# Expert weights in nine slots instead of six, three experts deep

## The chip, the cores and the metric
The kernel runs on one core of one Trainium2 chip. The metric is the device time in microseconds of one execution. Three runs of the kernel before took 3150.36, 3154.68 and 3155.96 us, median 3154.68 us.

## The reference, cut to what matters
The program computes two blocks over 512 tokens of width 1024, all in float32. The first block is a mixer (dilated attention and retention) followed by a mixture of experts: 8 groups of 8 experts, each token sent to 2 experts of one group. The second block has two more layers, which this change does not touch. The part that the change concerns is this:

```
hn = rms_norm(h, norm_moe_w)
group_p = softmax(hn @ w_group + b_group);  g_w, g_idx = top_k(group_p, 1)
exp_logits = hn @ w_expert + b_expert       # 64 experts, the 8 of the chosen group count
e_w, e_idx = top_k(softmax(sel_logits), 2)
...
hid = silu(xb @ w1[e]) * (xb @ w3[e])       # w1, w3: 1024 x 512
y   = hid @ w2[e]                           # w2: 512 x 1024
out = segment_sum(y * gate)                 # then added to h
```

Each expert has three weight matrices of 2 MB each (2048 KB), so all 64 experts together have 192 matrices.

## The kernel before, in words
The program is a sequence of stages. At the end of each stage TensorE, VectorE and ScalarE report with `next_stage`, GpSimd collects the reports and increments `stage_open`, and only then do the engines go on. SyncE (SP) is outside this: it issues nearly all weight loads, in one order written out by hand, and each load waits for semaphores of its own. SP stops at the first wait that is not yet fulfilled, and every later load stands behind it.

The stages around the change are these. The *rest* stage ends the mixer: its last two weight units, 22 and 23 (`w_out`), are multiplied on TensorE (line 1239), `h` is normed tile by tile, and ScalarE stores the normed tiles to `normed_rows` in DRAM (line 1208). A unit of weights lies in two of the four ring slots, even units in slots 0 and 2, odd units in 1 and 3; `release_unit` increments `unit_used` when TensorE has done with one. `stage_open` is 6 when the *route* stage opens and 7 when the *experts* stage opens. In the route stage VectorE picks the two experts of each token in a long chain of small operations (lines 1451 to 1534), with a short piece on TensorE; GpSimd scatters a table of slots to DRAM (line 1546), and ScalarE reads it back (line 1438).

In the experts stage each expert is computed for up to 32 rows. GpSimd gathers the rows by an indirect DMA (`gather`, issued two experts ahead, line 1620) and scatters the results (line 1625). TensorE transposes the rows (line 1656), multiplies by w1 and w3 (line 1664, `up_product`), then does the down product of the expert *before* (line 1680, w2), the transpose of the next rows, and the transposes of the hidden values (line 1671). The order inside the body of expert e is therefore: up e (w1, w3), down e-1 (w2), transpose rows of e+1, transpose hidden of e.

The weights are in `wide`, six slots of 2 MB, two experts deep: expert e uses slots 3*(e%2)+j for j = 0, 1, 2 (w1, w3, w2). Slots 0 to 3 lie in the same place as the ring, slot 4 is `xn`, slot 5 is `xnT`. SP issues in the order e, j (line 1611):

- slots 0 to 3 (all of expert 0 and w1 of expert 1) after `unit_used` 24, that is when the last ring unit has been used, and `rows_sent`;
- slots 4 and 5 after `stage_open` 7;
- from then on w1 of e waits for `pair_used` 2e-3 (the first w3 product of expert e-2), w3 of e for `pair_used` 2e-2 (the transpose of rows after it), and w2 of e for `down_used` e, which is incremented at the hidden transposes in the body of expert e-1, after the down product of e-2.

As w2 of e stands in front of w1 and w3 of e+1 in SP's order, and its wait is fulfilled last, the three loads w2 of e, w1 of e+1, w3 of e+1 leave together, at the hidden transposes in the body of expert e-1. In what follows this is called the burst. At that time the loads that are still under way are those of the burst before, which were issued one expert earlier.

All engines run `turns`: four bodies written out, then a loop of 15 turns with four bodies each. The stage's work buffers are in `arena`: the route stage's (class `G`) first and the experts' (class `E`) behind them.

Of the kernel before, what the change touches and what calls it, by code (L numbers as in the profile page):

```python
# [18 lines left out]
F32 = mybir.dt.float32  # L19
# [7 lines left out]
P = 128  # L27
D = 1024
# [107 lines left out]
def build(nc, t, const, out):  # L136
    ctx = ExitStack()
    with ctx:
# [14 lines left out]
        expert_loaded = [sem(f"expert_loaded{i}") for i in range(6)]  # L153
# [54 lines left out]
        with ExitStack() as plain:  # L208
            wide = plain.enter_context(nc.sbuf_tensor("wide", [P, 6, UNIT], F32))
# [1171 lines left out]

        class G:
            lay = Arena(arena)
# [28 lines left out]
            empty = lay(2 * BLOCKS).bitcast(I32)  # L1412

# [139 lines left out]
        U_EXPERTS = 24  # L1553
        PAR = 4
        SLOTS = 6
        assert 3 * PAR % SLOTS == 0 and U_EXPERTS % RING == 0 and EXPERTS % PAR == 0

        class E:
            lay = Arena(arena)
            lay.at = G.lay.at  # L1560
            table = lay(2 * BLOCKS).bitcast(I32)
            index = lay(4, 2).bitcast(I32)
            x = lay(2, D)
            xT = lay(2, KC, CAP)
            gate = lay(HID)
            up = lay(HID)
            gate_sum = lay(FC, CAP)
            up_sum = lay(FC, CAP)
            silu = lay(FC, CAP)
            hT = lay(FC, CAP)  # L1570
            y = lay(2, D)
# [13 lines left out]
        def turns(eng, body):  # L1585

            for b in range(PAR):
                body(0, b)
            with eng.Fori(1, EXPERTS // PAR) as it:
                for b in range(PAR):  # L1590
                    body(it, b)

        def expert_slot(b, j):
            return 3 * (b % 2) + j

        def expert_unit(k, cols):
            return wide[:, k].rearrange("p (c n) -> p c n", n=cols)

        def experts_sp(sp):
            def body(it, b):  # L1600
                e = it * PAR + b
                for j, src in enumerate(expert_weights(e)):
                    k = expert_slot(b, j)
                    if isinstance(it, int) and e < 2:
                        if k >= RING:
                            sp.wait_ge(stage_open, STAGES_BEFORE_EXPERTS)
                    elif j < 2:
                        sp.wait_ge(pair_used, e * 2 + (j - 3))
                    else:
                        sp.wait_ge(down_used, e)  # L1610
                    sp.dma_start(expert_unit(k, src.shape[2]), src).then_inc(expert_loaded[k], 16)  # L1611
            turns(sp, body)

        def wait_expert_unit(eng, it, b, j):

            eng.wait_ge(expert_loaded[expert_slot(b, j)], it * (8 * PAR) + 16 * (b // 2 + 1))

# [10 lines left out]
        def experts_pool(pool):  # L1628
            nc.gpsimd.tensor_copy(E.index[0:CAP, 0:2], E.table[0:CAP, 0:4].rearrange("p (e k) -> p e k", k=2)).then_inc(Z.index_copied, 1)
            pool.wait_ge(Z.index_copied, 1)  # L1630
            for b in range(2):
                gather(b, E.index[:, b]).then_inc(gathered[b], 16)

            def body(it, b):
                e = it * PAR + b

                wait_past(pool, scattered[b % 2], it * 32 + 16 * (b // 2))
                nc.gpsimd.tensor_copy(E.index[0:CAP, (b + 2) % 4], E.table[0:CAP, bass.ds(it * (2 * PAR) + 2 * (b + 2), 2)]).then_inc(Z.index_copied, 1)
                pool.wait_ge(Z.index_copied, e + 2)
                pool.wait_ge(Z.x_turned, e + 1)  # L1640
                pool.sem_inc(Z.waits_passed, 1)
                gather(b % 2, E.index[:, (b + 2) % 4]).then_inc(gathered[b % 2], 16)
                pool.wait_ge(Z.y_act, e + 1)
                pool.wait_ge(Z.y_dve, e + 1)
                pool.sem_inc(Z.waits_passed, 1)
                scatter(b % 2, E.index[:, b % 4]).then_inc(scattered[b % 2], 16)
            turns(pool, body)
            for s_ in scattered:
                pool.wait_ge(s_, 16 * EXPERTS // 2)
            for s_ in gathered:  # L1650
                pool.wait_ge(s_, 16 * (EXPERTS // 2 + 1))
# [42 lines left out]
        def experts_pe(pe):  # L1694
# [11 lines left out]
            def body(it, b):  # L1706
# [10 lines left out]
                pe.wait_ge(gathered[(b + 1) % 2], it * 32 + 16 * ((b + 1) // 2 + 1))  # L1717
# [13 lines left out]
            down(EXPERTS // PAR, 0, EXPERTS)[-1].then_inc(Z.down_ready, 1)  # L1731

        def experts_dve(v):
            def keep_y(it, b, e):

                v.wait_ge(Z.down_ready, e)
                s_ = (b + 1) % 2
                wait_past(v, scattered[s_], it * 32 + 16 * ((b - 1) // 2))
                keep_y_dve(s_).then_inc(Z.y_dve, 1)
# [17 lines left out]
            keep_y(EXPERTS // PAR, 0, EXPERTS)  # L1757

        def experts_act(a):
# [3 lines left out]
            def keep_y(it, b, e):  # L1763
# [3 lines left out]
                wait_past(a, scattered[s_], it * 32 + 16 * ((b - 1) // 2))  # L1767
# [15 lines left out]
            keep_y(EXPERTS // PAR, 0, EXPERTS)  # L1783
# [1022 lines left out]
        def _(sp):  # L2806
# [8 lines left out]
            sp.wait_ge(unit_used, FIRST_UNITS)  # L2815
            sp.wait_ge(rows_sent, 1)
# [205 lines left out]
```

## Time and profile before

| what | value |
|---|---|
| median of 3 runs | 3154.68 us |
| the profiled execution's own time | 3155.72 us |
| its span | 3153.9 us |
| experts' weight loads | 192 of 2048 KB each, median 13.0 us from issue to landing |
| PE busy, whole span | 2658.0 us (84%) |
| POOL, ACT, DVE busy | 27%, 28%, 37% |
| last chain: PE, DMA | 59%, 23% (22% of the span is `wide<-in_moe_w`) |

The page divides the span into 40 slices of 79 us. In the slices from 790 to 1780 us the DMA row stands at 9 and the GB/s row above 400, while PE stands at 7 or 8 tenths and the other engines below that. Everywhere else the GB/s row is between 44 and 140 and PE is at 9 for the most part. So the experts stage has another limit than the rest of the program. The DMA share of a stretch is the mean busy share of the 16 DMA engines; it can come out slightly over 1.

### The profile page before, as it was taken

The numbers are of one execution on the slowest core, as the hardware profiler recorded it, in microseconds if no ns is written. First come the engines' busy times: TensorE is split into PE (matmuls) and PEld (weight loads), VectorE is DVE, ScalarE is ACT, GpSimd is POOL, SyncE is SP. The second block draws the span as 40 slices with busy tenths as digits, with TensorE's granted clock in tenths as the row PEclk, the third lists the DMA queues.
The fourth block names the chain that finished last, engine by engine and source line by source line (L and its number), as shares of the span: only waits on it lengthen the run. The fifth ranks groups of instructions, "written<-read, shape, count | busy, mean of one in ns | idle before, by whom it ended". The sixth has DMA issues, their size and how long they took to land.

```text
span 3153.9 us, 34872 instructions
## 1 busy us (share of the span) xinstructions
PE 2658.0 (84%) x13364; PEld 1843.0 (58%) x13364; DVE 1154.2 (37%) x1957; ACT 867.9 (28%) x1581; POOL 856.5 (27%) x520
## 2 busy tenths in 40 slices
PE   6999999995777777777777569989999699899998
PEld 6987777884222222222222257678877577688876
DVE  4343735133111111111111257454443364644433
ACT  2333334231111111111111133533332324433332
POOL 2332333351111111111111122224444222234442
PEclk9999999997887788888888779899999799999999
DMA  3222112333999999999999731123322221122321
GB/s 132 81 87 100 62 61 81 104 107 140 384 412 408 411 407 409 410 409 405 407 405 407 293 104 44 54 64 97 98 90 80 86 81 54 51 77 87 107 81 67
DMA packets 134282, 586.82 MB, mean 186 GB/s; under 512 B 15200, under 2 KB 62608, under 8 KB 108304
## 3 DMA queue, kind: packets, MB, share of 16 engines
q1 hardware_dynamic: 117632, 553.57, 45.2%
q10 hardware_dynamic: 10000, 23.15, 2.1%
q0 software_dynamic: 6528, 8.44, 0.8%
q8 instruction: 81, 1.33, 0.2%
q14 instruction: 41, 0.34, 0.0%
HBM read 578.99 MB, written 14.78 MB: 188 GB/s over the span
## 4 chain that ended last, share of the span: by engine, by line
PE 59%; DMA 23%; DVE 8%; ACT 3%; issue 3%; POOL 1%; SPq 1%; POOLq 1%; ACTq 0%; PEldq 0%; PEld 0%; DVEq 0%
PE ps L329 36%; DMA wide<-in_moe_w 22%; PE ps L1239 7%; PE ps L1680 4%; PE ps L1664 3%; PE ps L577 1%; PE ps L1656 1%; POOL ring_r L307 1%; ACT ring_r L301 1%; PE ps L1046 1%; PE ps L548 1%; DVE xn L363 1%; SPq L1611 1%; PE ps L563 1%; DMA ring<-in_w_up 1%
## 5 line engine op out<-in xcount | busy, mean ns | idle before, releaser
L307 POOL TENSOR_TENSOR ring_r<-ring,ring_r 128x1024 fp32r<-128x1024 f32 (+2 forms) x288 | 698.9, 2458 | 1270.5 <-ACT ring_r L301 1270.5
L1664 PE MATMUL ps<-wide,arena 128*32 128x512 f32 x2048 | 349.0, 815 | 249.3 <-DMA wide<-in_moe_w 248.7
L329 PE MATMUL ps<-xnT_r,ring_r 128*128 128x512 f32 (+1 forms) x1664 | 496.0, 379 | 13.8 <-DVE xn_r L2406 7.4
L329 PE MATMUL ps<-ring_r,xnT_r 128*128 128x512 f32 (+1 forms) x1360 | 442.6, 397 | 30.4 <-POOLq L259 28.0
L329 PEld LDWEIGHTS ps<-xnT_r,ring_r 128*128 128x128 f32 x1664 | 308.5, 191 | 81.6 <-issue 19.9
L329 PE MATMUL ps<-ring_r,arena_r 128*128 128x512 f32 x1392 | 339.2, 401 | 14.3 <-DVE arena_r L2762 10.7
L329 PEld LDWEIGHTS ps<-ring_r,xnT_r 128*128 128x128 f32 x1360 | 288.8, 224 | 78.3 <-issue 28.8
L1664 PEld LDWEIGHTS ps<-wide,arena 128*32 128x32 f32 x2048 | 67.3, 129 | 451.1 <-DMA wide<-in_moe_w 270.9
L329 PE MATMUL ps<-xn_r,ring_r 128*128 128x512 f32 (+1 forms) x832 | 312.8, 376 | 0.0
L329 PEld LDWEIGHTS ps<-ring_r,arena_r 128*128 128x128 f32 x1392 | 264.8, 193 | 80.9 <-issue 25.5
L301 ACT ACTIVATE ring_r<-ring 128x1024 fp32r<-128x1024 f32 (+2 forms) x288 | 274.2, 1025 | 109.1 <-DMA ring<-in_w_down 62.0
L1625 POOL DMA_INDIRECT expert_rows<-arena x64 | 56.7, 886 | 808.1 <-DVE arena L1691 805.3
L1680 PE MATMUL ps<-wide,arena 128*32 128x512 f32 x1024 | 268.7, 672 | 1.3 <-issue 1.3
L1745 DVE COPY arena<-ps 128x512 f32<-128x512 f32 x64 | 44.3, 692 | 549.0 <-PE ps L1664 549.0
L1680 PEld LDWEIGHTS ps<-wide,arena 128*32 128x32 f32 x1024 | 69.9, 129 | 218.8 <-issue 218.8
L1688 ACT ACTIVATE arena<-ps 32x512 f32<-32x512 f32 x64 | 37.5, 586 | 566.5 <-PE ps L1680 566.5
L329 PEld LDWEIGHTS ps<-xn_r,ring_r 128*128 128x128 f32 x832 | 159.1, 191 | 26.4
L329 PE MATMUL ps<-ring_r,h_r 128*128 128x512 f32 (+1 forms) x424 | 167.9, 396 | 0.0
L2695 DVE SCALAR_TENSOR_TENSOR arena<-ps,arena 128x511 f32<-128x511 f32 x88 | 66.0, 750 | 262.1 <-ACT arena L2709 262.1
L2709 ACT ACTIVATE arena<-ps,arena 128x512 f32<-128x512 f32 x88 | 60.7, 690 | 304.0 <-PE ps L329 304.0
L1239 PE MATMUL ps<-ring_r,xnT_r 128*128 128x512 f32 x384 | 125.0, 396 | 2.9 <-POOLq L259 1.6
L1691 DVE COPY arena<-ps 32x512 f32<-32x512 f32 x64 | 43.7, 682 | 213.6 <-PE ps L1680 213.6
(339 smaller groups left out, 3232.8 us busy)
## 6 DMA issues: line engine op xcount, KB each, us to landing
wide<-in_moe_w SPq DMA_DIRECT2D x192, 2048.0 KB, 13.0
ring<-in_w_in SPq DMA_DIRECT2D x27, 2048.0 KB, 8.5
ring<-in_w_up SPq DMA_DIRECT2D x22, 2048.0 KB, 8.9
ring<-in_w_down SPq DMA_DIRECT2D x10, 2048.0 KB, 7.8
ring<-in_w_out SPq DMA_DIRECT2D x6, 2048.0 KB, 8.8
ring<-in_w_ret_branch SPq DMA_DIRECT2D x2, 2048.0 KB, 9.7
arena<-expert_rows ACTq DMA_DIRECT2D x4, 1024.0 KB, 10.1
attn_spill<-arena ACTq DMA_DIRECT2D x2, 1056.0 KB, 10.6
```

What stands on the lines that cost most here:

```text
L301: nc.scalar.activation(ring_r[:, 2 + q % 2, cols], ring[:, q % 2, cols], ACT.Copy).then_inc(half_high, 1)
L307: nc.gpsimd.tensor_tensor(ring_r[:, q % 2, cols], ring[:, q % 2, cols], ring_r[:, 2 + q % 2, cols].bitcast(F32), ALU.subtract).then_inc(ha ...
L329: ins = nc.tensor.matmul(bank, left, right, start=(start and k == 0), stop=(stop and k == 2))
L1239: ins = nc.tensor.matmul(ps[:, job_bank(n), 0:right.shape[1]], left, right, start=(x == 0), stop=(x == len(pairs) - 1))
L1625: return nc.gpsimd.indirect_dma_start(out=expert_rows, out_offset=bass.IndirectOffsetOnAxis(ap=index[0:CAP, 1:2], axis=0), in_=E.y[0:CAP, ...
L1664: res.append(nc.tensor.matmul(ps[g * CAP:(g + 1) * CAP, bank, :], xT[:, c, :], w[:, c, :], start=(c < 4), stop=(c >= KC - 4), tile_positio ...
L1680: return [nc.tensor.matmul(ps[half * CAP:(half + 1) * CAP, DOWN_BANK, :], E.hT[:, c, :], w[:, c, half * BANK:(half + 1) * BANK], start=(c ...
L1688: return nc.scalar.activation(E.y[0:CAP, into, 0:BANK], ps[0:CAP, DOWN_BANK, :], ACT.Copy)
L1691: return nc.vector.tensor_copy(E.y[0:CAP, into, BANK:], ps[CAP:2 * CAP, DOWN_BANK, :])
L1745: nc.vector.tensor_copy(E.up, ps[:, UP_BANK, :]).then_inc(Z.up_kept, 1)
L2695: link(nc.vector.scalar_tensor_tensor(out=acc[:, 1:], in0=bank[:, 0:S - 1], scalar=taps[:, 1:2], in1=acc[:, 1:], op0=ALU.mult, op1=ALU.add))
L2709: nc.scalar.activation(Y.acc[:, j % 2, s_], ps[:, UP_BANKS[n % 8], :], ACT.Copy, scale=Y.fconv[:, s_ * FB + j, FCONV - 1:FCONV]).then_inc( ...
```

## The change
`wide` gets a seventh slot (it lies over `rows`, which holds the route weights until the end of the rest stage), and slots 7 and 8 are the last 16384 words of a partition of `arena` (`late_slots`). To make room there, the experts' buffers now come first in `arena` and the route stage's buffers lie over those of them that only the experts stage writes. Expert e uses slots 3*(e%3)+j.

SP's loads before the experts stage are now nine instead of four: w1 and w2 of expert 0 after `unit_used` 23, w3 of expert 0 and w1 of expert 1 after `unit_used` 24, and five more (w3 and w2 of expert 1, all three of expert 2) after `stage_open` 6 and all four stores of `normed_rows` (`normed_stored` 64). From expert 3 on, w1 waits for `pair_used` 2e-5, w3 for 2e-4 and w2 for `down_used` e-1, each one expert earlier than before. The burst is thus w2 of e+1, w1 and w3 of e+2, at the hidden transposes in the body of expert e-1.

The four bodies written out stay, and the loop has 10 turns of six bodies each; the waits' numbers follow from that.

```diff
-        expert_loaded = [sem(f"expert_loaded{i}") for i in range(6)]
+        expert_loaded = [sem(f"expert_loaded{i}") for i in range(9)]
...
-            wide = plain.enter_context(nc.sbuf_tensor("wide", [P, 6, UNIT], F32))
+            wide = plain.enter_context(nc.sbuf_tensor("wide", [P, 7, UNIT], F32))
...
+            late_slots = arena[:, ARENA - 2 * UNIT:].rearrange("p (k n) -> p k n", k=2)
...
         class G:
-            lay = Arena(arena)
+            lay = Arena(arena, E.at)
...
-            for b in range(PAR):
+            for b in range(FIRST):
                 body(0, b)
-            with eng.Fori(1, EXPERTS // PAR) as it:
-                for b in range(PAR):
+            with eng.Fori(0, EXPERTS // PAR) as it:
+                for b in range(FIRST, FIRST + PAR):
                     body(it, b)
 
         def expert_slot(b, j):
-            return 3 * (b % 2) + j
+            return 3 * (b % AHEAD) + j
...
         def experts_sp(sp):
+            sp.wait_ge(unit_used, FIRST_UNITS - 1)
+            sp.wait_ge(rows_sent, 1)
+            load_expert(sp, 0, 0, 0)
+            load_expert(sp, 0, 0, 2)
+            sp.wait_ge(unit_used, FIRST_UNITS)
+            load_expert(sp, 0, 0, 1)
+            load_expert(sp, 1, 1, 0)
+            sp.wait_ge(stage_open, STAGES_BEFORE_EXPERTS - 1)
+            sp.wait_ge(normed_stored, 16 * NT)
+            load_expert(sp, 1, 1, 1)
+            load_expert(sp, 1, 1, 2)
+            for j in range(3):
+                load_expert(sp, 2, 2, j)
+
             def body(it, b):
                 e = it * PAR + b
-                for j, src in enumerate(expert_weights(e)):
-                    k = expert_slot(b, j)
-                    if isinstance(it, int) and e < 2:
-                        if k >= RING:
-                            sp.wait_ge(stage_open, STAGES_BEFORE_EXPERTS)
-                    elif j < 2:
-                        sp.wait_ge(pair_used, e * 2 + (j - 3))
+                if isinstance(it, int) and e < AHEAD:
+                    return
+                for j in range(3):
+                    if j < 2:
+                        sp.wait_ge(pair_used, e * 2 + (j - 2 * AHEAD + 1))
                     else:
-                        sp.wait_ge(down_used, e)
-                    sp.dma_start(expert_unit(k, src.shape[2]), src).then_inc(expert_loaded[k], 16)
+                        sp.wait_ge(down_used, e + (2 - AHEAD))
+                    load_expert(sp, e, b, j)
```

`AHEAD` is 3, `PAR` is 6 and `FIRST` is 4.

## Rows read from the trace of the kernel before

**Rows 1.** The page, part 2: GB/s in 40 slices of 79 us.
```profile
GB/s 132 81 87 100 62 61 81 104 107 140 384 412 408 411 407 409 410 409 405 407 405 407 293 104 44 54 64 97 98 90 80 86 81 54 51 77 87 107 81 67
```

**Rows 2.** The page, part 6: issues, KB each, median us to landing.
```profile
wide<-in_moe_w SPq DMA_DIRECT2D x192, 2048.0 KB, 13.0
```

**Rows 3.** Windows: busy us by engine; last are PE clock, DMA share, GB/s.
```profile
744.00:760.00 16.00, 7.09 (x36) 6.76 (x35) 7.14 (x48) 1.72 (x3) 2.72 (x3) 0.64 1.00 423
760.00:780.00 20.00, 0.00 (x0) 0.00 (x0) 13.26 (x37) 0.00 (x0) 7.97 (x7) 0.50 0.02 4
...
798.00:802.00 4.00, 4.00 (x31) 1.04 (x23) 0.13 (x1) 0.60 (x1) 0.04 (x1) 0.80 0.27 72
820.00:1760.00 940.00, 692.74 (x3810) 247.19 (x3808) 176.71 (x299) 112.11 (x240) 120.89 (x180) 0.82 0.99 409
```

**Rows 4.** Chain of waits, end of the route stage: start us, us, what.
```profile
780.24 2.11 DMA slot_table<-arena
...
786.82 8.32 DMA arena<-normed_rows,arena
```

**Rows 5.** Timeline, PE: start, us, work; in brackets idle before, releaser.
```profile
796.74 5.05 PE L1664 MATMUL ps<-wide,arena 128*32 128x512 f32 x32 [0.47 <-ACT arena L1685]
...
811.86 1.23 PE L1671 MATMUL ps<-cst,arena 128*128 128x128 f32 x8
...
823.04 1.06 PE L1656 MATMUL ps<-cst,arena 32*128 32x32 f32 x8 [2.97 <-DMA arena<-normed_rows,arena]
```

**Rows 6.** Chain of waits: w3 of an odd expert landed, and its first product started.
```profile
833.04 2.98 PE ps L1664 x16
...
1651.36 1.92 PE ps L1664 x16
...
1682.27 1.92 PE ps L1664 x16
...
1777.27 1.92 PE ps L1664 x16
```

**Rows 7.** Windows around late bursts, columns as in Rows 3.
```profile
981.00:985.00 4.00, 4.00 (x26) 2.27 (x22) 0.87 (x2) 0.97 (x2) 0.20 (x1) 1.00 0.82 348
1304.00:1314.00 10.00, 8.23 (x33) 1.85 (x33) 0.69 (x1) 0.28 (x1) 0.00 (x0) 0.62 1.01 426
1314.00:1318.00 4.00, 4.00 (x34) 2.34 (x32) 2.27 (x4) 1.28 (x3) 1.50 (x3) 1.00 0.73 238
1318.00:1328.00 10.00, 7.51 (x51) 3.34 (x48) 1.88 (x3) 1.57 (x3) 1.13 (x2) 1.00 1.00 424
1708.00:1712.00 4.00, 2.65 (x23) 1.02 (x22) 1.58 (x3) 0.97 (x3) 2.01 (x3) 1.00 0.87 291
```

**Rows 8.** Timelines of PE and SP at a slow and a fast body.
```profile
1305.77 3.64 PE L1664 MATMUL ps<-wide,arena 128*32 128x512 f32 x16 [2.14 <-DMA wide<-in_moe_w]
...
1315.35 1.56 SPq L1611 DMA_DIRECT2D wide<-in_moe_w  x3
...
1658.04 18.71 SPq L1611 DMA_DIRECT2D wide<-in_moe_w  x6
```

**Rows 9.** Landing of the gathers, by their line (count; min/median/max).
```profile
L1620 POOL DMA_INDIRECT arena<-normed_rows,arena x66: 897/936/949, 786.8 to 1789.3; - x66
...
DMA to landing us min/median/max: 2.0/7.3/9.1
```

**Rows 10.** Chain of waits, the last scatter of the experts stage.
```profile
1792.96 2.49 DMA expert_rows<-arena
```

**Rows 11.** End of the rest stage: unit 23 starts on PE; last store of rows.
```profile
709.73 11.17 PE L1239 MATMUL ps<-ring_r,arena_r 128*128 128x512 f32 x48 [0.26 <-issue]
...
739.22 0.33 ACTq L1208 DMA_DIRECT2D normed_rows<-xn  x1
```

**Rows 12.** The stores of the normed rows, by their line.
```profile
DMA to landing us min/median/max: 2.6/7.2/15.3
```

**Rows 13.** Timeline, SP: the first six loads, in one merged piece.
```profile
735.50 50.98 SPq L1611 DMA_DIRECT2D wide<-in_moe_w  x6
```

More of the change, by code:

```diff
@@ L1380, in build @@
         spill_info = small[:, 408:408 + SPILL + 1].bitcast(I32)
+        U_EXPERTS = 24
+        AHEAD = 3
+        PAR = 2 * AHEAD
+        FIRST = EXPERTS % PAR
+        assert U_EXPERTS % RING == 0 and FIRST >= AHEAD
+        class E:
+            lay = Arena(arena)
+            table = lay(2 * BLOCKS).bitcast(I32)
+            index = lay(PAR, 2).bitcast(I32)
+            x = lay(2, D)
+            at = lay.at
+            xT = lay(2, KC, CAP)
+            gate = lay(HID)
+            up = lay(HID)
+            gate_sum = lay(FC, CAP)
+            up_sum = lay(FC, CAP)
+            silu = lay(FC, CAP)
+            hT = lay(FC, CAP)
+            y = lay(2, D)
+            late_slots = arena[:, ARENA - 2 * UNIT:].rearrange("p (k n) -> p k n", k=2)
+            assert lay.at <= ARENA - 2 * UNIT
         class G:
-            lay = Arena(arena)
+            lay = Arena(arena, E.at)
             w = rows[:, 2, 0:KC * ROUTES].rearrange("p (c n) -> p c n", c=KC)
@@ L1412, in build @@
             empty = lay(2 * BLOCKS).bitcast(I32)
+            assert lay.at <= ARENA - 2 * UNIT
         def load_routes(a):
@@ L1547, in route_pool @@
                                                  in_=G.pair_i[:, i, k, :], in_offset=None).then_inc(table_out, 16)
[L1553 to L1571, printed above, removed]
         X_BANK, GATE_BANK, UP_BANK, GATE_T_BANK, UP_T_BANK, DOWN_BANK = range(6)
@@ L1599, in experts_sp, with load_expert @@
-        def experts_sp(sp):
+            home = wide[:, k] if k < 7 else E.late_slots[:, k - 7]
+            return home.rearrange("p (c n) -> p c n", n=cols)
+        def load_expert(sp, e, b, j):
+            src = expert_weights(e)[j]
+            k = expert_slot(b, j)
+            sp.dma_start(expert_unit(k, src.shape[2]), src).then_inc(expert_loaded[k], 16)
+        def experts_sp(sp):
+            sp.wait_ge(unit_used, FIRST_UNITS - 1)
[11 more added lines that the diff above has]
+                load_expert(sp, 2, 2, j)
@@ L1635, in body @@
                 e = it * PAR + b
-                wait_past(pool, scattered[b % 2], it * 32 + 16 * (b // 2))
-                nc.gpsimd.tensor_copy(E.index[0:CAP, (b + 2) % 4], E.table[0:CAP, bass.ds(it * (2 * PAR) + 2 * (b + 2), 2)]).then_inc(Z.index_copied, 1)
+                wait_past(pool, scattered[b % 2], it * (8 * PAR) + 16 * (b // 2))
+                nc.gpsimd.tensor_copy(E.index[0:CAP, (b + 2) % PAR], E.table[0:CAP, bass.ds(it * (2 * PAR) + 2 * (b + 2), 2)]).then_inc(Z.index_copied, 1)
                 pool.wait_ge(Z.index_copied, e + 2)
@@ L1641, in body @@
                 pool.sem_inc(Z.waits_passed, 1)
-                gather(b % 2, E.index[:, (b + 2) % 4]).then_inc(gathered[b % 2], 16)
+                gather(b % 2, E.index[:, (b + 2) % PAR]).then_inc(gathered[b % 2], 16)
                 pool.wait_ge(Z.y_act, e + 1)
@@ L1645, in body @@
                 pool.sem_inc(Z.waits_passed, 1)
-                scatter(b % 2, E.index[:, b % 4]).then_inc(scattered[b % 2], 16)
+                scatter(b % 2, E.index[:, b % PAR]).then_inc(scattered[b % 2], 16)
             turns(pool, body)
@@ L1716, in body @@
                     down(it, b, e)[-1].then_inc(Z.down_ready, 1)
-                pe.wait_ge(gathered[(b + 1) % 2], it * 32 + 16 * ((b + 1) // 2 + 1))
+                pe.wait_ge(gathered[(b + 1) % 2], it * (8 * PAR) + 16 * ((b + 1) // 2 + 1))
                 pe.sem_inc(Z.pe_passed, 1)
@@ L1730, in experts_pe @@
             turns(pe, body)
-            down(EXPERTS // PAR, 0, EXPERTS)[-1].then_inc(Z.down_ready, 1)
+            down(EXPERTS // PAR, FIRST, EXPERTS)[-1].then_inc(Z.down_ready, 1)
         def experts_dve(v):
@@ L1737, in keep_y @@
                 s_ = (b + 1) % 2
-                wait_past(v, scattered[s_], it * 32 + 16 * ((b - 1) // 2))
+                wait_past(v, scattered[s_], it * (8 * PAR) + 16 * ((b - 1) // 2))
                 keep_y_dve(s_).then_inc(Z.y_dve, 1)
@@ L1756, in experts_dve @@
             turns(v, body)
-            keep_y(EXPERTS // PAR, 0, EXPERTS)
+            keep_y(EXPERTS // PAR, FIRST, EXPERTS)
         def experts_act(a):
@@ L1766, in keep_y @@
                 s_ = (b + 1) % 2
-                wait_past(a, scattered[s_], it * 32 + 16 * ((b - 1) // 2))
+                wait_past(a, scattered[s_], it * (8 * PAR) + 16 * ((b - 1) // 2))
                 keep_y_act(s_).then_inc(Z.y_act, 1)
@@ L1782, in experts_act @@
             turns(a, body)
-            keep_y(EXPERTS // PAR, 0, EXPERTS)
+            keep_y(EXPERTS // PAR, FIRST, EXPERTS)
         def spills(eng, body):
@@ L2814, in _ @@
                 sp.dma_start(ring[:, u % 2].rearrange("p (c n) -> p c n", n=src.shape[2]), src).then_inc(unit_loaded[u % 2], 16)
-            sp.wait_ge(unit_used, FIRST_UNITS)
-            sp.wait_ge(rows_sent, 1)
             experts_sp(sp)
```

3 lines of the change are left out of this document (1 added, 2 removed).

## The prediction, made before the changed kernel had run
> **What bounds the kernel now.** I read the 40 slices first. The reader is to see there that the GB/s row is three to five times as high in the experts stage as elsewhere and nearly level, about 400 to 412 over some 980 us [rows 1]. A level row at the top of its range, with a DMA share of 0.99 over 940 us [rows 3], says that the weight loads set the time of this stage. Then the chain of waits at a point that comes back in each pair of experts, the landing of w3 of an odd expert: 833.04 and 1777.27 us are 30 pairs apart [rows 6], so a pair takes 944.2 / 30 = 31.47 us, an expert 15.74 us and a 2 MB load 5.246 us. TensorE has no part in that pace: it is busy 692.7 of 940 us [rows 3].
>
> Two places in the stage are not level. The first is its start. The engines load four units up to 760 us, then the DMA stands still (share 0.02, 760 to 780 us) while the routes are computed, and at 798 to 802 us it nearly does so again (72 GB/s) [rows 3], since slots 4 and 5 have landed and TensorE has only just begun to free slots (first product at 796.74 us [rows 5]). The second I found by going through the stage in windows of 1 us. Twelve stretches of 4 us have a DMA share of 0.88 or less; the first, the last and a deep one stand in [rows 7]. At the deep one the DMA moves 426 GB/s, then 238, then 424. Beside it stands what happened [rows 8]: TensorE started the w3 product at 1305.77 us at its lower clock (the window's mean is 0.62 [rows 7], 0.50 is the level of 1.2 GHz), got to the hidden transposes slowly, and SP issued the burst at 1315.35 us, 9.6 us after that w3 had landed. With the clock high it is 1658.04 - 1651.36 = 6.7 us [rows 6, 8]. Three loads of 5.2 us are ordered per burst, and from them go the 9.6 us, the start-up of the new loads and the time between the last byte and the landing of the old ones: nothing is left when TensorE is slow. So the stage is bound by loads, with small holes that a late burst makes.
>
> **The change part by part.** The sum is made against the profiled execution (3155.72 us, span 3153.9).
>
> *Five loads moved ahead of the stage.* Unit 22 is done before 709.73 us [rows 11], so w1 and w2 of expert 0 (two loads, some 10 us) run then beside a DMA that is nearly idle [rows 1]. The other two of the old four are issued at 735.50 us [rows 13] as before. With two instead of four loads in front, the last store of rows (issued 739.22 us [rows 11]; the longest of the four took 15.3 us behind four loads [rows 12]) should land at about 750, at the worst 754.5 us. The five new loads start then: at 423 GB/s [rows 3] one takes 4.96 us, five 25 us, and with 2 us of start-up they end near 777, at the worst 782 us. They lie beside the chain on VectorE, which needs no DMA until 770 us. The last table scatter goes out at 780.24 us [rows 4], after they end, so I cost their contention at 0. If they ran to 782, this scatter would take some 7 us as the contended gathers do [rows 9], not 2.11 [rows 4]: 5 us back. When the stage opens, nine units are there, where before six were there by the time that TensorE began. From its first product on the same thing happens in both: slots come free in the same rhythm, with the same hole at the start, and what remains is 183 loads, not 186. Three loads at 5.246 us: **-15.7 us**. It is three and not five, because before, two units moved from 786 to 798 us, when the DMA will now stand idle with all slots full.
>
> *The first gather.* The gather of expert 0's rows took 8.32 us, beside the loads into slots 4 and 5 [rows 4, 13], and TensorE waited for it. In the new order nothing else is under way then. A transfer of the same kind in an idle DMA is the last scatter of the stage, 2.49 us [rows 10]; the shortest gather took 2.0 us [rows 9]. I take 2.5: TensorE starts at 790.9 instead of 796.74 us, **-5.8 us**. The bounds are 0 (it stays at 8.3) and -6.3.
>
> *Slots one expert deeper.* The burst no longer competes with the landing of the loads just before it: when it is late by the 3 us between 9.6 and 6.7, there are three more loads queued or landed. So the holes go. Their price, against 424 GB/s: the twelve stretches sum up to 10.7 us of load time that was lost (4 us x (1 - GB/s / 424) for each, as 1.8 us for the deepest and 0.7 us for the first [rows 7]). A second way: a pair without a hole is 1682.27 - 1651.36 = 30.91 us [rows 6] against 31.47 on average, 0.56 us x 30 = 17 us. That one is picked from the short end, so I take **-12 us**, near the count; the bounds are 0 and -17. What is late next is again the DMA, now without a break: TensorE can go faster than it, see the first rival.
>
> *At no cost.* The loop of six bodies with 10 turns instead of 15: the same instructions run, and what an engine loses at a turn is covered by TensorE's 26% of free time [rows 3]. The waits are renumbered, not added. SP's new waits stand in front of nothing but expert loads: `unit_used` 23 is reached before 24, and `stage_open` 6 and the stores come before the next place at which SP had to wait anyway. The other arrangement of `arena` changes no operation. I bound these together at 1 us either way. The tail after the last w3 (1777.27 us) is TensorE's own work and the last scatter [rows 6, 10]: it moves as a whole.
>
> Sum: -15.7 - 5.8 - 12 = -33.5 us, 3155.7 - 33.5 = 3122.2 us in the profiled execution. This one lies 1.0 us over the median of the runs shown, so the forecast for the median is 3121 us.
>
> *Two rules of the Trainium skill weighed.* The DMA moves 409 GB/s over the stage, and 424 to 426 beside a hole [rows 3, 7]. The Trainium skill, DMA: Bandwidth & Descriptors, section Where 436 GB/s comes from, says that for transfers from HBM to SBUF the HBM's share of a core, about 358 GB/s, is what binds, and its table of one core alone has 425 GB/s for 16 MB. By the first there would be no room for a faster pace and the third term would be 0; by the second it would be as I have it. The trace speaks for the second.
>
> **The rivals.** *The gathers become the bound (slower).* With three more loads queued in front, a gather might take longer. The row that shows the loop at its limit is at 811.86 to 823.04 us: TensorE came to the next transposes of rows 11.2 us later and had waited 2.97 us for a gather [rows 5]; an expert can thus take no less than some 12.2 us while a gather takes about 8.3. To fall behind the old pace of 15.74 us it would need a gather of about 8.3 + 3.5 = 11.8 us. Were it the 15.3 us that the store of rows took behind four loads [rows 12], an expert would take 12.2 + 7.0 = 19.2 us, and 61 experts 61 x 3.5 = 213 us more, less the 21.5 us of the first two terms: some 3345 us. It decides from a gather of about 12.1 us on, where it eats up the 21.5 us as well. For it speaks that store. Against it: the gather behind two loads took 8.3 us [rows 4], and the median in the stage, with on average 13.0 / 5.2 = 2.5 loads under way [rows 2], is 7.3 and the most 9.1 [rows 9], so it does not grow with the queue. The Trainium skill, DMA: Bandwidth & Descriptors, section Queues, rings and completion order, says that each DMA engine goes round its queues packet by packet; by this a gather on GpSimd's queue pays for the packet in front and not for the depth of SP's queue, and this rival would be worth 0.
>
> *The holes stay.* If the dips in [rows 7] come from something else than the late burst (the scatter and gather that go out in the same 3 us, say), only the first two terms count: 3154.7 - 21.5 = 3133 us. For it: the scatter and the gather really fall into them. Against it: they go out with every expert, and there are twelve holes in sixty.
>
> *Only the count of loads helps.* The gather stays at 8.3 us, because the five loads begin late or run long and it meets them, and the holes stay: 3154.7 - 15.7 = 3139 us.
>
> *The change does not do what it says.* SP could reach the five loads only near the end of the route stage, for instance when the stores land much later. Then nine units are there no earlier than six before, and the stage only gains its steadier pace or nothing: within 6 us of 3155.
>
> **How the numbers follow.** The forecast 0.66 (own range 3110 to 3128: the third term between 6 and 17 us, the other two within 5); the holes stay 0.17 (3133); only the count 0.08 (3139); no effect 0.04; gathers bound 0.05 (3345). The range of 3110 to 3138 us holds the first two cases and the edge of the third. 0.2% is 6.3 us, about what a measurement of this kernel can tell from no change. The first three cases and a part of the fourth are faster by more: 0.92; within it 0.03; slower 0.05.
>
> **What would show each step right or wrong.** The windows: from 709 to 721 us a DMA share well over 0.5, from 750 to about 777 us a full one, then nothing until TensorE has begun; if the full stretch runs past 782 us, the first term is smaller. The chain: the gather of expert 0 at about 2.5 us and the first product near 791 us; at 797 the second term was wrong. The landings of w3, two experts apart: 30.9 to 31.0 us each and none of 32; and the DMA share without windows under 0.9 at the bursts, while TensorE's clock goes up and down as before. If the holes are there with the nine slots too, the third step was wrong. The landing time of the weight loads should go from 13 to about 25 us or more with the pace the same or better: loads wait in the queue. If TensorE waits for gathers in the steady state, the first rival holds.

## The result, and the profile after

The changed kernel takes 3129.91 us (median of 5 runs, 3118.92 to 3132.97) against 3154.68 us for the kernel before beside it (median of 5, 3146.96 to 3157.39). The ratio is 0.9916, 95% interval 0.9891 to 0.9941. A second set of runs of the same kernel, in the experiments below, gives 0.9929 (0.9916 to 0.9943). By the medians it is faster by 21 to 25 us; the forecast for the median was 33.5 us faster, 3121 us. So 3129.91 us lies in the range of 3110 to 3138 us, but outside the forecast's own range of 3110 to 3128 us, and nearer to the rival "the holes stay" (3133 us). The profiled execution took 3120.85 us, span 3119.0 us, which lies close to the forecast 3122.2 us, but by luck, as the account below shows.

The page of the changed kernel, GB/s in 40 slices (78 us each) and the issues of weight loads (KB each, median us to landing). Slots 7 and 8 appear as `arena`:

```profile
GB/s 133 81 82 101 69 61 68 107 120 270 308 416 417 418 416 418 414 412 413 408 409 416 231 102 49 55 76 87 102 88 81 87 82 55 55 81 81 108 81 68
...
wide<-in_moe_w SPq DMA_DIRECT2D x150, 2048.0 KB, 32.1
arena<-in_moe_w SPq DMA_DIRECT2D x42, 2048.0 KB, 30.5
```

The slice before the stage has 270 GB/s where it had 140 [rows 1], and a load waits 32.1 us in the queue where it waited 13.0 [rows 2]. Windows of the changed kernel (busy us by engine; last PE clock, DMA share, GB/s):

```profile
709.00:721.00 12.00, 11.74 (x52) 9.43 (x51) 2.08 (x4) 2.73 (x4) 2.21 (x1) 1.00 0.77 303
750.00:777.00 27.00, 6.23 (x28) 6.04 (x28) 17.50 (x64) 0.21 (x1) 4.75 (x4) 0.50 0.92 377
788.00:800.00 12.00, 8.89 (x55) 4.06 (x56) 0.74 (x2) 1.69 (x4) 2.89 (x4) 0.62 0.22 54
820.00:1740.00 920.00, 679.67 (x3807) 243.52 (x3806) 176.03 (x298) 112.16 (x239) 119.80 (x178) 0.82 1.00 414
1728.00:1744.00 16.00, 12.67 (x72) 4.46 (x68) 2.95 (x5) 1.88 (x4) 2.01 (x3) 0.82 0.92 382
1744.00:1760.00 16.00, 13.18 (x76) 4.36 (x70) 3.19 (x6) 1.88 (x4) 2.01 (x3) 0.83 0.27 110
```

The two early loads run from about 711 us, the five from about 753 us, and the standstill now comes after them. In the steady part the DMA moves 414 GB/s, not 409 [rows 3]. The last row is the one to look at: for the last 16 us of the loads the DMA share is 0.27, as much as if some four of the 16 engines worked, while TensorE still waits for loads. In the kernel before, the share stays at 1 to within a few us of the end:

```profile
1760.00:1776.00 16.00, 12.74 (x64) 4.37 (x64) 2.95 (x5) 2.29 (x5) 2.02 (x3) 0.72 1.01 415
1776.00:1784.00 8.00, 6.73 (x43) 2.77 (x44) 1.37 (x2) 1.02 (x3) 0.00 (x0) 1.00 0.23 97
```

The chain of waits of the changed kernel (start us, us, what), which answers to [rows 4, 6]; 862.10 us is w3 of expert 6, the 20th load in SP's order, 1757.78 us w3 of expert 63, the 191st:

```profile
781.43 2.10 DMA slot_table<-arena
...
787.93 2.66 DMA arena<-normed_rows,arena
...
862.10 3.52 PE ps L1693 x16
...
1757.78 1.92 PE ps L1693 x16
```

And its timeline of TensorE at the stage's start, and the landing of its 66 gathers, against [rows 5, 9]:

```profile
790.64 1.09 PE L1685 MATMUL ps<-cst,arena 32*128 32x32 f32 x8 [29.88 <-DMA arena<-normed_rows,arena]
792.20 6.04 PE L1693 MATMUL ps<-wide,arena 128*32 128x512 f32 x32 [0.47 <-ACT arena L1714]
```

```profile
L1649 POOL DMA_INDIRECT arena<-normed_rows,arena x66: 897/936/947, 787.9 to 1769.8; - x66
...
DMA to landing us min/median/max: 2.0/7.1/8.5
```

The gather of expert 0 takes 2.66 us instead of 8.32, and TensorE starts at 792.20 instead of 796.74 us (all of the program up to there runs 1.1 us later). But from the 20th to the 191st load 895.7 us pass, 5.238 us a load. Before it was 5.246 [rows 6], and between the same two loads as here 5.251, where w3 of expert 6 starts at 879.42 us:

```profile
879.42 3.64 PE L1664 MATMUL ps<-wide,arena 128*32 128x512 f32 x16 [3.33 <-DMA wide<-in_moe_w]
```

With the second trace of the changed kernel (5.245, below) that is worth 1 to 2 us in 171 loads: the pace has hardly changed.

### The profile page after: what moved, and what is told of

The parts are those of the page before. It is cut to its first block, busy times and chain, and to the rows that moved or that the text cites. A ratio compares the mean times of both kernels' runs of the same rounds, so it can differ in the third digit from the quotient of the medians.

```text
span 3119.0 us, 34828 instructions
## 1 busy us (share of the span) xinstructions
PE 2631.7 (84%) x13364; PEld 1830.7 (59%) x13364; DVE 1151.3 (37%) x1957; ACT 868.4 (28%) x1581; POOL 859.0 (28%) x520
## 4 chain that ended last, share of the span: by engine, by line
PE 58%; DMA 25%; DVE 8%; ACT 3%; issue 2%; POOL 1%; SPq 1%; POOLq 1%; ACTq 0%; PEldq 0%; DVEq 0%; PEld 0%
PE ps L329 38%; DMA wide<-in_moe_w 24%; PE ps L1239 7%; PE ps L1709 3%; PE ps L1693 2%; PE ps L577 1%; PE ps L1046 1%; DVE xn L363 1%; PE ps L548 1%; ACT ring_r L301 1%; PE ps L1685 1%; POOL ring_r L307 1%; PE ps L563 1%; PE ps L2473 1%; PE ps L1037 1%
## 5 line engine op out<-in xcount | busy, mean ns | idle before, releaser
L1693 PE MATMUL ps<-wide,arena 128*32 128x512 f32 x1712 | 288.7, 809 | 196.3 <-DMA wide<-in_moe_w 195.7
L1654 POOL DMA_INDIRECT expert_rows<-arena x64 | 56.7, 886 | 793.3 <-DVE arena L1720 790.6
L1693 PEld LDWEIGHTS ps<-wide,arena 128*32 128x32 f32 x1712 | 55.9, 131 | 355.8 <-DMA wide<-in_moe_w 204.0
L1709 PE MATMUL ps<-wide,arena 128*32 128x512 f32 x688 | 175.7, 657 | 1.3 <-issue 1.3
L1709 PEld LDWEIGHTS ps<-wide,arena 128*32 128x32 f32 x688 | 45.4, 125 | 139.3 <-issue 139.3
L2791 DVE TENSOR_TENSOR arena_r<-arena,arena_r 128x512 fp32r<-128x512 f32 x44 | 66.0, 1530 | 147.0 <-ACT arena_r L2784 147.0
## 6 DMA issues: line engine op xcount, KB each, us to landing
wide<-in_moe_w SPq DMA_DIRECT2D x150, 2048.0 KB, 32.1
```

What stands on the lines that cost most here:

```text
L1654: return nc.gpsimd.indirect_dma_start(out=expert_rows, out_offset=bass.IndirectOffsetOnAxis(ap=index[0:CAP, 1:2], axis=0), in_=E.y[0:CAP, ...
L1693: res.append(nc.tensor.matmul(ps[g * CAP:(g + 1) * CAP, bank, :], xT[:, c, :], w[:, c, :], start=(c < 4), stop=(c >= KC - 4), tile_positio ...
L1709: return [nc.tensor.matmul(ps[half * CAP:(half + 1) * CAP, DOWN_BANK, :], E.hT[:, c, :], w[:, c, half * BANK:(half + 1) * BANK], start=(c ...
L2791: nc.vector.tensor_tensor(Y.act_low[:, b], Y.act[:, b], Y.act_high[:, b % HIGH_BLOCKS].bitcast(F32), ALU.subtract).then_inc(Z.act_low, 1)
```

## The experiments

After the first result I had two theories. **H** is the prediction's: late bursts cost 12 us, and with the third expert of depth the pace falls to 5.15 us. **P**: the pace of landings is set by something that no depth of the queue touches. A load has landed when each of the 16 DMA engines has moved its part, so if one engine is slower than the rest it sets the pace, and the others run ahead as far as the slots allow. That would explain a mean rate that rises while loads land no faster, and the long thin end. The Trainium skill, DMA: Bandwidth & Descriptors, section Why a DMA increments its semaphore by 16 and not by 1, says that only the full count of 16 means that all data has landed; what was seen fits.

The packed traces settle P, for they hold the time of each of a load's 16 increments, though not which engine made it. If P is right, the first of the 16 must come ever further ahead of the last until the slots stop it. In the changed kernel the first comes 4.6 us ahead between 800 and 900 us (median), 8.6 in the next 100 us, then 13.1 and 18.0, and from 1200 us on it stays between 20 and 22 us. In the kernel before it stays between 3 and 6 us all along (read from its w2 loads: for most others an increment is missing in the trace). The last load of the changed kernel has ten of its 16 parts in by 1745.1 us and its last part at 1762.6 us, which is the thin end. So the depth of three experts went into a longer lead of the engines that were ahead anyway. Nor is it one engine that is behind: in the median load of the changed kernel seven parts come more than 16 us before the last, two 11 to 12 us and the others 8 us or less.

To compare stages I use the first start of an up product and the last start of a matmul of a down product, from the instructions that read `wide`:

| kernel | stage from, to (us) | median us (runs) | ratio to before, 95% |
|---|---|---|---|
| before | 796.7, 1790.8 | 3154.68 (5) | 1 |
| changed | 792.2, 1771.2 | 3129.91 (5) | 0.9916 (0.9891 to 0.9941) |
| a0_again | 792.5, 1772.0 | 3130.65 (5) | 0.9929 (0.9916 to 0.9943) |
| e1_depth_only | 798.0, 1784.2 | 3145.13 (11) | 0.9982 (0.9973 to 0.9991) |
| e2_six_early | 790.6, 1785.7 | 3148.43 (11) | 0.9988 (0.9979 to 0.9998) |
| e4_six_reordered | 797.8, 1788.4 | 3146.60 (11) | 0.9985 (0.9976 to 0.9994) |
| g1_nine_spread | 794.1, 1754.3 | 3114.42 (4) | 0.9878 (0.9862 to 0.9893) |
| g2_six_spread | 800.3, 1779.9 | 3138.24 (5) | 0.9950 (0.9937 to 0.9964) |
| h1_gather_no_rows | 792.8, 1728.1 | 3084.59 (4) | 0.9777 (0.9762 to 0.9792) |
| e5_nine_reordered | 791.1, 1768.9 | 3129.22 (5) | 0.9915 (0.9900 to 0.9930) |
| e7_seven_early | 797.1, 1774.6 | 3137.16 (6) | 0.9934 (0.9919 to 0.9949) |
| e3_no_first_pair | 797.1, 1777.9 | 3136.52 (6) | 0.9934 (0.9920 to 0.9949) |
| e6_six_bodies | 799.5, 1796.7 | 3150.73 (12) | 0.9982 (0.9972 to 0.9992) |
| g3_nine_spread_reordered | 791.7, 1752.3 | 3111.43 (5) | 0.9856 (0.9840 to 0.9872) |

The kernels before beside them had medians of 3151.71 (a0 to e4), 3154.58 (g1, g2, h1, e5) and 3154.09 us (the last four).

**The changed kernel again (a0_again).** No edit.

> The changed kernel itself, once more, for a second profile and more rounds. In the two traces so far the experts stage ends 19.5 us earlier (start of the last down product 1786.04 against 1766.56 us), while the span is 34.9 us shorter: 15.4 us of it come after the stage, where the programs are the same. Theory P (a landing pace that no queue depth changes; 5.24 us per load in both traces): the stage's end at 1766 to 1768 us again, and the 15.4 us are the spread of single executions, so the difference of the medians lies at 20 to 26 us. Theory H (my prediction: late bursts cost 12 us): the stage's pace is 5.15 to 5.20 us per load in this trace, and the whole gain about 33 us.

The stage ends at 1772.0 us, within 1 us of the first trace, and the span is 3132.7 us, not 3119.0. From the last down product to the end of the span the three traces have 1363.1 (before), 1347.8 (changed) and 1360.7 us (again), with the same program there. So the first trace had some 13 us of luck behind the stage. From w3 of expert 6 to w3 of expert 63 a load takes 5.245 us, where the first trace had 5.238:

```profile
860.48 1.92 PE ps L1693 x16
...
1757.33 3.64 PE ps L1693 x16
```

H had 5.15 to 5.20 for this; P's account of the stage stands.

**Depth without the early loads (e1_depth_only).** The first pair leaves with the other two at `unit_used` 24, and the five leave at `stage_open` 7:

```diff
-            sp.wait_ge(unit_used, FIRST_UNITS - 1)
+            sp.wait_ge(unit_used, FIRST_UNITS)
             sp.wait_ge(rows_sent, 1)
-            load_expert(sp, 0, 0, 0)
-            load_expert(sp, 0, 0, 2)
-            sp.wait_ge(unit_used, FIRST_UNITS)
-            load_expert(sp, 0, 0, 1)
+            for j in range(3):
+                load_expert(sp, 0, 0, j)
             load_expert(sp, 1, 1, 0)
-            sp.wait_ge(stage_open, STAGES_BEFORE_EXPERTS - 1)
-            sp.wait_ge(normed_stored, 16 * NT)
+            sp.wait_ge(stage_open, STAGES_BEFORE_EXPERTS)
```

> Nine slots, three deep, but the first four loads leave where they did before and the other five only when the experts stage opens. The early fetch is undone, the depth is kept. Theory P: the DMA runs without a break from 786 us on, so what goes is the standstill at 798 to 802 us and the dip at 812 to 816 us, some 5 us together; the gather of expert 0 stays at about 8.3 us; the pace stays 5.24 us per load; in all 4 to 7 us faster than before. Theory H: the same and 12 us for the late bursts, 16 to 20 us faster, with a pace of 5.15 us per load.

Stage end 6.6 us earlier, the median 6.6 us less, by the ratio 5.7 us. From w3 of expert 5 (17th load) to the 191st it takes 912.06 us, 5.242 us each:

```profile
860.30 1.92 PE L1690 MATMUL ps<-arena 128*32 128x512 f32 x16 [3.31 <-DMA arena<-in_moe_w]
...
1772.36 1.92 PE L1690 MATMUL ps<-wide,arena 128*32 128x512 f32 x16 [1.78 <-DMA wide<-in_moe_w]
```

That is P; the depth is worth no more than the hole at the stage's start.

**Early loads without the depth (e2_six_early).** In the kernel before, slots 4 and 5 are loaded in the route stage:

```diff
                         if k >= RING:
-                            sp.wait_ge(stage_open, STAGES_BEFORE_EXPERTS)
+                            sp.wait_ge(stage_open, STAGES_BEFORE_EXPERTS - 1)
+                            sp.wait_ge(normed_stored, 16 * NT)
```

> Six slots, two deep, as before, but slots 4 and 5 are loaded in the route stage. Both theories: only the gather of expert 0 gets shorter, 8.3 to about 2.6 us, TensorE's first product comes 5 to 6 us earlier and everything behind it with it: 5 to 6 us faster. The rival, that each load taken out of the stage is worth its 5.24 us: 10 us or more faster.

The gather takes 2.73 us, the stage ends 5.1 us earlier, the ratio says 3.8 us (0.6 to 6.6). Two loads taken out of the stage gave nothing beyond the gather; the rival of 10 us or more is out.

**The late bursts removed with six slots (e4_six_reordered).** The body of SP's loop issues w1 and w3 of e (j is 0 and 1 only), then w2 of e-1:

```diff
...
-                    else:
-                        sp.wait_ge(down_used, e)
-                    sp.dma_start(expert_unit(k, src.shape[2]), src).then_inc(expert_loaded[k], 16)
+                    load_one(sp, e, b, j)
+                if not (first and e < 3):
+                    sp.wait_ge(down_used, e - 1)
+                    load_one(sp, it * PAR + (b - 1), b - 1, 2)
```

> Six slots, two deep, nothing early, but SP issues w1 and w3 of expert e+1 as soon as their slots are free and w2 of expert e behind them, so no burst of three waits for the hidden transposes: two of the three loads leave some 7 us earlier. The holes of the DMA at late bursts should go without a seventh slot. Theory H: 11 to 17 us faster, landing pace 5.15 us per load. Theory P (the landing pace is set by something that the holes don't touch, the slowest of the 16 DMA engines): no window under 0.9 at the bursts either, but the pace stays 5.24 us and the time is 0 to 4 us less, from the start of the stage.

This was the straight test of the third term. The windows of 4 us with a share of 0.88 or less fell from twelve to five, the mean rate rose to 411 GB/s, and the pace stayed: TensorE's waits for w2, in bodies 60 experts apart, are 944.3 us apart, 5.246 us a load.

```profile
820.00:1760.00 940.00, 681.54 (x3830) 244.07 (x3826) 177.32 (x300) 112.64 (x240) 120.91 (x180) 0.86 1.00 411
```

```profile
832.36 3.63 PE L1688 MATMUL ps<-wide,arena 128*32 128x512 f32 x16 [1.51 <-DMA wide<-in_moe_w]
...
1776.66 5.32 PE L1688 MATMUL ps<-wide,arena 128*32 128x512 f32 x16 [3.00 <-DMA wide<-in_moe_w]
```

By the medians it is 5 us faster all the same (ratio 0.9985, a size that the last control below makes doubtful; the stage ends 2.4 us earlier), where H had 11 to 17. H is refuted: the holes were real, but no load landed sooner without them. They were idle time of engines that had run ahead: here the first of a load's 16 increments comes 12.6 us before the last (median), where it was 4.6 us in the kernel before, and the last comes no sooner.

**Which work makes an engine slow (g1_nine_spread, g2_six_spread).** New theory **S**: the rows of the gathers lie unevenly over the engines. An expert has 16 tokens on average in a block of 32 rows, filled from row 0. If an engine carries two neighbouring rows, those of the low rows have two in every transfer and those of the high rows none. Two operations on VectorE spread the tokens:

```diff
+            link(nc.vector.tensor_scalar(G.by_group, G.place, CAP / 2 - 0.5, 1.0 - CAP, ALU.is_gt, ALU.mult))
+            link(nc.vector.scalar_tensor_tensor(out=G.place, in0=G.place, scalar=2.0, in1=G.by_group, op0=ALU.mult, op1=ALU.add))
             link(nc.vector.tensor_scalar(G.place, G.place, float(BLOCKS), None, ALU.mult))
```

> The changed kernel, and in the route stage two more VectorE operations (some 0.8 us) that put the r-th token of an expert not into row r of its block of 32 but into row 2r (r under 16) or 2r-31. Theory S (my new one: each of the 16 DMA engines carries two neighbouring rows of a gather or scatter; tokens fill a block from row 0, 16 of 32 on average, so the engines of the low rows carry two rows of each transfer and those of the high rows none; the loaded ones have 24 x 0.613 + 4 x 0.159 = 15.35 us of packets per expert against 14.7, and they set the landing pace of 15.7 us): with the rows spread the slowest engine has 0.32 us less per expert, 61 x 0.32 = 19 us off the changed kernel, pace 5.13 us per load, and the long tail of the DMA at the stage's end (share 0.2 to 0.4 over 16 us) shrinks to a few us. Rival N (one engine is slow by itself, or the rows are dealt out round robin): no gain, 0 to +2 us, the tail stays.

15.5 us less than the changed kernel by the medians, 12 to 16 by the ratios, where S had 19. The 20th and the 191st load are 880.1 us apart, 5.147 us each, and the mean rate is 420 GB/s. The end of the loads is less thin (share 0.53 in the last 16 us against 0.27), so some unevenness is left. The increments say the same: the lead of the first over the last grows by some 2 us in 100 us, where it grew by 4 to 5 us in the changed kernel until the slots stopped it. No trace names the engine of a row, so the two neighbouring rows are what fits and are not shown; rows dealt out one by one (rival N) would have gained nothing.

```profile
862.36 2.82 PE L1695 MATMUL ps<-wide,arena 128*32 128x512 f32 x16 [3.05 <-DMA wide<-in_moe_w]
...
1742.45 1.92 PE L1695 MATMUL ps<-wide,arena 128*32 128x512 f32 x16 [2.43 <-DMA wide<-in_moe_w]
```

```profile
820.00:1700.00 880.00, 648.02 (x3698) 234.78 (x3700) 170.10 (x288) 108.40 (x231) 116.62 (x174) 0.83 1.01 420
...
1728.00:1744.00 16.00, 13.57 (x80) 4.54 (x74) 2.95 (x5) 1.88 (x4) 2.02 (x3) 0.82 0.53 221
```

The same two operations in the kernel before:

> The same two operations in the kernel before (six slots, two deep). Theory S: the slowest engine gets 0.32 us per expert shorter here too, but with two experts' depth a late burst now may hold up all engines: 10 to 19 us faster than before; what is missing from 19 us is what the late bursts cost when the engines are even. Rival N: no gain.

16.3 us less than before, with a pace of 5.152 us from the 11th to the 191st load. The two kernels gain about the same and their paces lie within 0.012 us, so even with the engines more even the late bursts cost at most some 2 us.

```profile
837.78 1.92 PE L1666 MATMUL ps<-wide,arena 128*32 128x512 f32 x16 [1.67 <-DMA wide<-in_moe_w]
...
1765.17 3.41 PE L1666 MATMUL ps<-wide,arena 128*32 128x512 f32 x16 [3.35 <-DMA wide<-in_moe_w]
```

**The gathers' own price (h1_gather_no_rows).** In the changed kernel all gathers of the loop take their indices from a tile that holds only an out-of-range row:

```diff
...
-                gather(b % 2, E.index[:, (b + 2) % PAR]).then_inc(gathered[b % 2], 16)
+                gather(b % 2, E.none[:, 0]).then_inc(gathered[b % 2], 16)
```

> The changed kernel, but from the third expert on the gathers point at rows out of range, so they move no row (the experts compute with zeros or old rows; the output is not the reference's). Scatters stay. Theory S: the slowest engine has 2 x 0.159 = 0.32 us per expert less, 19 us faster than the changed kernel, pace 5.13 us per load. If gathers are dealt out evenly over the engines: 0.16 us per expert, 10 us. If one engine is slow for another reason, for example by its place or by instruction fetches: 10 us or less, and the run-ahead of the others as before (the low DMA share at the stage's end).

45 us less than the changed kernel by the medians (44 to 48 by the ratios), not 19. The pace is 4.999 us (854.9 us for 171 loads), the rate 428 GB/s:

```profile
859.72 3.64 PE L1695 MATMUL ps<-wide,arena 128*32 128x512 f32 x16 [3.30 <-DMA wide<-in_moe_w]
...
1714.58 2.77 PE L1695 MATMUL ps<-wide,arena 128*32 128x512 f32 x16 [1.95 <-DMA wide<-in_moe_w]
```

```profile
820.00:1700.00 880.00, 657.86 (x3812) 241.44 (x3816) 175.88 (x298) 111.98 (x239) 119.79 (x178) 0.86 1.01 428
```

An expert takes 3 x (5.238 - 4.999) = 0.72 us less. By S that is two gathered rows, so 0.36 us each, more than twice the 0.159 us of a row's own packet. S had the place right and the size wrong; spreading the rows gave 3 x (5.238 - 5.147) = 0.27 us. The packed traces show where the rest lies: the packets of the weight loads, 16 KB each, take longer beside a gather. Between 820 and 1700 us 1743 of 21818 of them take over 660 ns in the changed kernel and 20 of 22739 here, and the mean falls from 629 to 614 ns. An engine moves 24 such packets per expert, so that is 0.35 us; with two rows of 0.159 it makes 0.67 us, an estimate that comes near the 0.72. The scattered rows are still there in this kernel, so they hardly slow the packets of the loads. Why a gathered row does was not tried.

**What the early loads are worth, one by one (e7_seven_early, e3_no_first_pair).** The last two of the nine wait for the stage:

```diff
-            for j in range(3):
-                load_expert(sp, 2, 2, j)
+            load_expert(sp, 2, 2, 0)
+            sp.wait_ge(stage_open, STAGES_BEFORE_EXPERTS)
+            load_expert(sp, 2, 2, 1)
+            load_expert(sp, 2, 2, 2)
```

> The changed kernel, but the last two of the nine loads (w3 and w2 of expert 2) wait until the experts stage opens, so seven are early instead of nine. My accounting (two loads move in the 12 us between the stage's opening and TensorE's first free slot anyway, but they stand beside the gather of expert 0): the gather takes about 8 us again, TensorE starts 5 to 6 us later with nine loads there, 5 to 6 us slower than the changed kernel. Rival (each load taken out of the stage is worth 5.24 us, and the gather on top): 10 to 16 us slower.

The gather takes 7.86 us, TensorE starts at 797.1 us, the stage ends 3.4 us later, and the median is 7 us over the changed kernel's. The ratios are nearer to each other (0.9934 against 0.9916 and 0.9929, 2 to 6 us), so the size is loose, but nothing points to 10 to 16 us. The accounting holds: two of the five loads bring no more than the gather, not 5.24 us each.

```profile
787.65 7.86 DMA arena<-normed_rows,arena
```

Then the nine without the first pair (all four at `unit_used` 24):

> The changed kernel, but the first two loads don't leave at unit_used 23; all four leave at unit_used 24 as before the change. The four then run to about 760 us, the stores of rows land at about 755 us, and the five run from there to about 787 us. By my accounting they still end about when the stage opens: the last table scatter and the read of the table meet them (2.1 and 1.7 us become some 4 to 7 us together more), the gather does not or hardly. 3 to 8 us slower than the changed kernel. Rival (the order of the early loads is hidden altogether): 0 to 2 us.

6 to 7 us slower by the medians (2 to 6 by the ratios), and the stage ends 6.7 us later. The last table scatter meets the five loads and takes 6.61 us instead of 2.10, while the gather stays short: the two loads at 711 us were needed to finish in time.

```profile
781.63 6.61 DMA slot_table<-arena
...
792.70 2.84 DMA arena<-normed_rows,arena
```

**Controls (e5_nine_reordered, e6_six_bodies, g3_nine_spread_reordered).** w2 behind the next w1 and w3, with nine slots:

> The changed kernel with SP's order of the reordered kernel of six slots: w1 and w3 of expert e+1, then w2 of e. In the steady state the queue is deep enough, so nothing changes there. At the start the dip at 810 to 812 us, where SP stood at w2 of expert 3, goes: 1 to 3 us faster than the changed kernel by theory P; by theory H (late bursts cost time) not more either, since nine slots have removed them.

0.7 us less than the changed kernel, the stage's end 2.3 us earlier: not told apart from nothing. The loop of six bodies and the new order of the arena alone:

> Six slots, two deep, all loads when they were before the change; only the loop of six bodies and the new order of the buffers in the arena are kept. Both theories: no change against the kernel before, within 2 us.

The ratio 0.9982 (0.9972 to 0.9992) says 3 to 9 us faster, which neither theory had. Its trace shows no gain: the stage runs from 799.5 to 1796.7 us, 3 us longer than before, and behind it come 1352.1 us, where the profiles of the other kernels have 1348 to 1363. Whether these runs happened to be short behind the stage, or something in the program's layout helps there, stays open. It also means that ratios of 0.9982 to 0.9988 here are no proof of a gain without the trace. Last, both edits on the changed kernel:

> The changed kernel with both: tokens spread over the rows of their block, and w2 behind the next expert's w1 and w3 in SP's order. The reordering gave 0 to 1 us by itself; with even engines it should give no more. So the time of the kernel with spread rows alone, 3114 us against a kernel before of 3154 us, within 3 us.

3111.43 us, 43 us under the kernel before and the best version found that computes the reference; against the spread rows alone (3114.42) the step is within the noise.

## Why the prediction was right in its range and wrong in one term

**Which limit.** Right: the stage is bound by loads, TensorE waits for them in every body from expert 3 on before and from expert 6 on in the changed kernel, and the first rival (gathers as the bound) did not come: the gathers' median went from 7.3 to 7.1 us while a load's landing went from 13.0 to 32.1 us. The Trainium skill's rule of the round by packets (DMA: Bandwidth & Descriptors, Queues, rings and completion order) agrees with these two numbers.

**Three loads out of the stage, -15.7 us.** Right. From the first product to the landing of the last w3 it is 965.6 us where it was 980.5, 14.9 us less. That it is not five was shown by the kernel with seven early loads, and that nothing comes of it without slots by the early loads with six.

**The first gather, -5.8 us.** Right: 8.32 to 2.66 us, -5.7. That the early loads end before the table scatter was right too, and with little to spare: the last of the nine has landed at 780.8 us and the scatter goes out at 781.43; without the first pair the scatter paid 4.5 us (the prediction said 5 us for that case).

**The holes, -12 us.** Wrong, this is the step that failed: "So the holes go. Their price, against 424 GB/s". The holes did go in part, from twelve stretches to five in the steady part, and 414 GB/s were moved instead of 409, but a load landed every 5.238 to 5.245 us instead of 5.246 to 5.251, worth 1 to 2 us. The price was wrong, because a hole in the mean share of 16 engines is the idle time of those that are ahead: a load has landed with the last of its 16 parts, and that one came no sooner. The five holes that were left are the prediction's own sign against this step, and they bear the same mark: the first stands at 1388 us (1293 us in the second trace), after the lead had stopped growing. Nor does the step before it hold, that "nothing is left when TensorE is slow": three loads of 5.2 us less 9.6 us leave some 6 us, and no row showed that the rest takes that long. The second estimate, from a pair of 30.91 us [rows 6], took a short interval in a noisy series for the undisturbed pace. The second rival, "the holes stay", had nearly the right number (3133 us) for a wrong reason: it wanted another cause for the holes than the late bursts, but most of them went when the bursts came earlier (e4), and no time was won.

**No cost elsewhere.** Not told apart from nothing: with the loop of six bodies and the new arena alone the stage was 3 us longer in its one trace, where the prediction had 1 us, while the times were 3 to 9 us shorter.

The sum without the third term is 21.5 us, 3133 us; measured were 21 to 25 us, 3130 us. That the measured time lies in the range of 3110 to 3138 us is owed to the two first terms and to a range wide enough to hold a rival. In the profiled execution the stage ended 19.6 us earlier and the rest came behind the stage, where nothing was changed.

## What to carry to other kernels

When loads bound a stage, read the pace from landings (the instruction that waits for the same load in each turn), not from the mean GB/s or the mean share: depth can raise the mean while the slowest engine sets the pace. A thin end of the loads, a share well under 1 for longer than one load takes, is a sign of uneven engines; then look for small transfers that always fall on the same ones, as half-filled gathers do, and spread them. Here the early loads were worth the loads still missing when the first slot comes free, and the wait for the gather beside them, no more.

## What the runs showed of the hardware

Small gathers beside large loads are dear: 16 rows of 4 KB on average per expert are 1% of the bytes of an expert's weights, and without them a load takes 4.6% less (4.999 against 5.238 us). By spreading the same rows over the block, with no byte less, 1.7% came back (5.147 us). Half of that price is in the loads' own packets (629 against 614 ns in the mean). With the DMA otherwise idle a gather takes 2.66 us, beside loads 7.1 us in the median and 8.5 at most. Depth of the queue gave the faster engines a lead (20 us instead of 5) and the loads no pace.
